# Hybrid streaming encoder on one core: post-norm scales in halves, the last tile of squares added by TensorE, the next input's first tile in halves of the tokens

## What is computed

```
def rmsnorm(x, g):
    y = xf * lax.rsqrt(jnp.mean(xf * xf, axis=-1, keepdims=True) + EPS)
    return y * g
# trunk_layer
    h = rmsnorm(x, g_norm[0])            # norm 0
    ...                                  # three mixing branches, gates
    x = x + rmsnorm(merged @ w_out, g_norm[1])   # norm 3 of the kernel
    h = rmsnorm(x, g_norm[2])                    # norm 4
    ...                                  # cross-attention into 256 memory tokens
    x = x + rmsnorm(ox @ w_xo, g_norm[3])        # norm 5
    h = rmsnorm(x, g_norm[4])                    # norm 6
    u = jnp.square(jax.nn.relu(h @ w_up)) @ w_down
    x = x + rmsnorm(u, g_norm[5])                # norm 7
```

## Time and profile before

| | |
|---|---|
| median of 3 runs | 2743.57 us (2743.19 to 2744.48) |
| profiled execution, its own time | 2743.87 us |
| its span | 2742.0 us |
| mean granted TensorE clock | 0.966 |
| PE busy | 2551.7 us (93%) |
| PEld busy | 2386.0 us (87%) |
| DVE, ACT, POOL busy | 1045.0, 707.3, 1210.9 us |

### The profile page before, as it was taken

How to read it: one execution, slowest core, us unless ns; L and a number is a source line. 1 busy time by engine, 2 the same in 40 slices (tenths; PEclk the granted TensorE clock), 3 DMA queues, 4 the chain that set the end, 5 groups by cost and what they waited for, 6 DMA issues and landing times.

```text
span 2742.0 us, 43279 instructions
## 1 busy us (share of the span) xinstructions
PE 2551.7 (93%) x18670; PEld 2386.0 (87%) x18670; DVE 1045.0 (38%) x1596; ACT 707.3 (26%) x1571; POOL 1210.9 (44%) x700
## 2 busy tenths in 40 slices
PE   8899999998988899999998999999998887999997
PEld 7878977997888789999898789689888887999997
DVE  5442222478623341221373411324786144211223
ACT  2053133135312430010121522322253134210111
POOL 3312510665465245665543034126643732565663
PEclk9999999999999999999999999999999998999998
DMA  5313410330242123323234133113202421223321
GB/s 178 111 38 102 109 41 16 85 90 24 77 125 85 39 62 88 91 85 89 81 101 120 39 89 91 42 32 85 74 24 93 130 80 32 77 85 89 90 85 56
DMA packets 354533, 214.59 MB, mean 78 GB/s; under 512 B 22316, under 2 KB 347240, under 8 KB 353704
## 3 DMA queue, kind: packets, MB, share of 16 engines
q1 hardware_dynamic: 320632, 179.86, 23.1%
q10 hardware_dynamic: 33712, 31.97, 3.7%
HBM read 196.09 MB, written 15.71 MB: 77 GB/s over the span
## 4 chain that ended last, share of the span: by engine, by line
PE 83%; DVE 8%; ACT 4%; issue 3%; POOL 2%; DMA 0%; ACTq 0%; SPq 0%; DVEq 0%; POOLq 0%
PE psum L719 20%; PE psum L717 20%; PE psum L718 20%; PE psum L788 2%; PE psum L827 2%; PE psum L729 2%; PE psum L1110 1%; PE psum L998 1%; POOL w_lo L652 1%; PE psum L921 1%; PE psum L747 1%; PE psum L749 1%; PE psum L748 1%; DVE square_sum_and_rs L2020 1%; PE psum L762 1%
## 5 line engine op out<-in xcount | busy, mean ns | idle before, releaser
L650 POOL CAST w_hi<-w_raw 128x1024 fp32r<-128x1024 f32 x318 | 337.7, 1062 | 1382.5 <-PE psum L719 1204.9
L652 POOL TENSOR_TENSOR w_lo<-w_raw,w_hi 128x1024 fp32r<-128x1024 f32 x318 | 811.6, 2552 | 25.5
L717 PE MATMUL psum<-h_hi,w_hi 128*128 128x272 f32 x2720 | 791.1, 291 | 18.9 <-POOL w_lo L652 15.1
L719 PE MATMUL psum<-h_hi,w_lo 128*128 128x272 f32 x2720 | 788.4, 290 | 0.0
L718 PE MATMUL psum<-h_lo,w_hi 128*128 128x272 f32 x2720 | 783.8, 288 | 0.0
L717 PEld LDWEIGHTS psum<-h_hi,w_hi 128*128 128x128 f32 x2720 | 513.9, 189 | 24.0 <-issue 20.9
L718 PEld LDWEIGHTS psum<-h_lo,w_hi 128*128 128x128 f32 x2720 | 514.4, 189 | 0.7 <-issue 0.5
L719 PEld LDWEIGHTS psum<-h_hi,w_lo 128*128 128x128 f32 x2720 | 512.8, 189 | 0.0
L717 PE MATMUL psum<-r_hi,w_hi 128*128 128x272 f32 x1696 | 494.2, 291 | 6.2 <-DVE hE L2114 3.3
L719 PE MATMUL psum<-r_hi,w_lo 128*128 128x272 f32 x1696 | 495.8, 292 | 0.0
L718 PE MATMUL psum<-r_lo,w_hi 128*128 128x272 f32 x1696 | 491.8, 290 | 0.0
(11 more groups left out here) (380 smaller groups left out, 3593.7 us busy)
## 6 DMA issues: line engine op xcount, KB each, us to landing
w_raw<-in_w_in SPq DMA_DIRECT2D x116, 512.0 KB, 3.8
w_raw<-in_w_up SPq DMA_DIRECT2D x64, 512.0 KB, 4.0
w_raw<-in_w_down SPq DMA_DIRECT2D x64, 512.0 KB, 3.9
w_raw<-in_w_branch SPq DMA_DIRECT2D x24, 512.0 KB, 3.4
w_raw<-in_w_out SPq DMA_DIRECT2D x16, 512.0 KB, 3.9
x_kept<-x SPq DMA_DIRECT2D x2, 2176.0 KB, 8.9
x<-x_kept SPq DMA_DIRECT2D x2, 2176.0 KB, 9.7
fKc<-in_cache_fox_k ACTq DMA_DIRECT2D x4, 1024.0 KB, 7.8
```

Source lines behind the costliest of these rows:

```text
L650: nc.gpsimd.tensor_copy(w_hi[:, at % SPLIT, :], raw[:, at % RAW, :]).then_inc(high_split, 1)
L652: nc.gpsimd.tensor_tensor(w_lo[:, at % SPLIT, :], raw[:, at % RAW, :], w_hi[:, at % SPLIT, :].bitcast(F32), ALU.subtract).then_inc(weights ...
L717: pe.matmul(dst, whi[:, k, :], hi[:, k, c0:c1], start=k == 0, stop=False)
L719: last = pe.matmul(dst, wlo[:, k, :], hi[:, k, c0:c1], start=False, stop=k == kt - 1)
```

## The change

A unit is now a tile of x, or half of tile 0: `UNITS` has 9 of them (NU), tile 0 in two halves of 272 tokens and seven whole tiles. The counts of `x_ready`, `h_hi_ready` and `h_lo_ready` and the offsets XG0 to H_PARTS follow. `POSTS` names the norms of the outputs.

1. For norms 3, 5 and 7 DVE adds the squares of tiles 0 to 6. TensorE adds tile 7 with two more products by the ones, into the same banks, after it has multiplied `acc`.
2. For the same norms ACT makes Ln and Exp of the first half of the tokens and then of the second, and `rs_ready` counts each.
3. `post`, `x_parts`, `x_low` and `norm_products` take tile 0 in halves. ACT squares tile 0 whole, after its second half. This holds for the first input of the program (norm 0 of layer 0) too.

```diff
+        UNITS = [(0, slice(0, HALF)), (0, slice(HALF, NT))] + [(t, slice(0, NT)) for t in range(1, KT)]
+        NU = len(UNITS)
+        POSTS = (3, 5, 7)
+        RS_AT = [k + 1 + sum(j <= k for j in POSTS) for k in range(len(NORMS))]
...
-        SQUARES = {0: S["sqx"], 4: sq, 6: sq}
+        SQUARES = {0: S["sqx"], 3: sq, 4: sq, 5: S["sqx"], 6: sq, 7: S["sqx"]}
...
-            for t in range(KT):
-                pe.wait_ge(h_lo_ready, since(h_lo_ready, base + t + 1))
+            for u, (t, tokens_of) in enumerate(UNITS):
+                pe.wait_ge(h_lo_ready, since(h_lo_ready, base + u + 1))
                 for name, G, (whi, wlo) in zip(names, banks, split):
                     for a in range(2):
                         c = slice(a * HALF, (a + 1) * HALF)
+                        if not tokens_of.start <= c.start < tokens_of.stop:
+                            continue
...
-                if t < KT // 2:
+                if u and t < KT // 2:
                     square_tile(pe, k, t)
...
         def stat(pe, k):
             pe.wait_ge(square_sum_ready, since(square_sum_ready, k + 1 - sum(j < k for j in PE_SUMS)))
+            whole = k not in POSTS
             for a in range(2):
                 dst = bank_free(pe, ("stat", k, a))
-                pe.matmul(dst[:, 0:HALF], ones, acc[:, a * HALF:(a + 1) * HALF], start=True, stop=True) \
-                    .then_inc(fill_sem(("stat", k, a)), 1)
+                last = pe.matmul(dst[:, 0:HALF], ones, acc[:, a * HALF:(a + 1) * HALF], start=True, stop=whole)
+                if whole:
+                    last.then_inc(fill_sem(("stat", k, a)), 1)
+            if not whole:
+                pe.wait_ge(square_ready, since(square_ready, SQ0[k] + KT))
+                for a in range(2):
+                    pe.matmul(bank_of(("stat", k, a))[:, 0:HALF], ones, SQUARES[k][:, KT - 1, a * HALF:(a + 1) * HALF],
+                              start=False, stop=True).then_inc(fill_sem(("stat", k, a)), 1)
...
-                emptied(act, ("stat", k, 1)), emptied(act, ("stat", k, 0))
-                exp(rs, acc, scale=-0.5).then_inc(rs_ready, 1)
+                    if k in POSTS:
+                        emptied(act, name)
+                        exp(rs[:, a * HALF:(a + 1) * HALF], acc[:, a * HALF:(a + 1) * HALF], scale=-0.5) \
+                            .then_inc(rs_ready, 1)
...
-                v.wait_ge(rs_ready, since(rs_ready, k + 1))
-                for t in range(KT + 2):
-                    if t < KT:
+                for i in range(NU + 2):
+                    if i < NU:
+                        t, c = UNITS[i]
+                        if i < 2:
+                            v.wait_ge(rs_ready, since(rs_ready, RS_AT[k] - 1 + i))
                         n[0] += 1
-                        V.scalar_tensor_tensor(tmp[:, t, :], U[:, t, :], gT(gcol + t, gcol + t + 1), rs,
+                        V.scalar_tensor_tensor(tmp[:, t, c], U[:, t, c], gT(gcol + t, gcol + t + 1), rs[:, c],
                                                ALU.mult, ALU.mult).then_inc(vector_chain, 1)
...
-                square_add(v, 7, S["sqx"], KT - 1)
```

More of the change, by code:

```diff
@@ L486, in hybrid_encoder @@
         PER_LAYER = [
-            (square_ready, sum(NORMS)), (square_sum_ready, len(NORMS) - len(PE_SUMS)), (rs_ready, len(NORMS)),
-            (h32_ready, KT), (h_hi_ready, H_PARTS), (h_lo_ready, H_PARTS), (x_ready, 3 * KT),
+            (square_ready, sum(NORMS)), (square_sum_ready, len(NORMS) - len(PE_SUMS)), (rs_ready, RS_AT[-1]),
+            (h32_ready, KT), (h_hi_ready, H_PARTS), (h_lo_ready, H_PARTS), (x_ready, 3 * NU),
             (cqn_ready, 1), (rope_ready, 3), (row_max, 68), (sample_probs, 4), (o_hi_ready, 19),
@@ L1259, in rs_of @@
                                          bias=eps[:, 0:1], scale=1.0 / features).then_inc(empty_sem(name), 1)
-                emptied(act, ("stat", k, 1)), emptied(act, ("stat", k, 0))
-                exp(rs, acc, scale=-0.5).then_inc(rs_ready, 1)
+                    if k in POSTS:
+                        emptied(act, name)
+                        exp(rs[:, a * HALF:(a + 1) * HALF], acc[:, a * HALF:(a + 1) * HALF], scale=-0.5) \
+                            .then_inc(rs_ready, 1)
+                if k not in POSTS:
+                    emptied(act, ("stat", k, 1)), emptied(act, ("stat", k, 0))
+                    exp(rs, acc, scale=-0.5).then_inc(rs_ready, 1)
             def h_high(act):
@@ L1269, in x_parts @@
             def x_parts(act, k, base, gcol, hi):
-                for t in range(KT):
+                for u, (t, c) in enumerate(UNITS):
                     if base is not None:
-                        act.wait_ge(x_ready, since(x_ready, base + t + 1))
-                    nc.scalar.activation(hi[:, t, :], x[:, t, :], ACT.Copy, scale=gT(gcol + t, gcol + t + 1)) \
+                        act.wait_ge(x_ready, since(x_ready, base + u + 1))
+                    nc.scalar.activation(hi[:, t, c], x[:, t, c], ACT.Copy, scale=gT(gcol + t, gcol + t + 1)) \
                         .then_inc(h_hi_ready, 1)
+                    if u == 0:
+                        continue
                     nc.scalar.activation(SQUARES[k][:, t, :], x[:, t, :], ACT.Square).then_inc(square_ready, 1)
@@ L1672, in layer @@
                 emptied(act, ("vec",), l=l - 1 if l else "in")
-                x_parts(act, 0, -KT if l else None, V_NORM, r_hi)
+                x_parts(act, 0, -NU if l else None, V_NORM, r_hi)
                 rs_of(act, 0, D_MODEL)
@@ L1706, in square_sum @@
             def square_sum(v, k, tiles):
-                for t in range(1, NORMS[k]):
+                for t in range(1, NORMS[k] - (k in POSTS)):
                     square_add(v, k, tiles, t)
@@ L1955, in dve_mla @@
                         gate(v, "kpe")
-                    v.wait_ge(rs_ready, since(rs_ready, k + 1))
+                    v.wait_ge(rs_ready, since(rs_ready, RS_AT[k]))
                     for t in range(nt):
@@ L2133, in dve_cross @@
                 post(v, 3, V_NORM + KT, sq, XG4, V_NORM + 2 * KT, h_hi, h_lo, layer_now[0])
-                v.wait_ge(rs_ready, since(rs_ready, 5))
+                v.wait_ge(rs_ready, since(rs_ready, RS_AT[4]))
                 for m in range(4):
@@ L2147, in dve_mlp @@
                 v.wait_ge(DMA["out"], since(DMA["out"], 32))
-                v.wait_ge(rs_ready, since(rs_ready, 7))
+                v.wait_ge(rs_ready, since(rs_ready, RS_AT[6]))
                 for g in range(MLP_GROUPS):
@@ L2256, in _ @@
                 layer_now[0] = DEPTH - 1
-                pe.wait_ge(x_ready, since(x_ready, 2 * KT + 4 * c + 4))
+                pe.wait_ge(x_ready, since(x_ready, 2 * NU + 4 * c + 5))
                 layer_now[0] = "out"
@@ L2301, in _ @@
             layer_now[0] = 0
-            for t in range(KT):
+            for t in range(NU):
                 x_low(v, t, XG0, V_NORM, r_hi, r_lo, 0)
```

25 lines of the change are left out of this document (14 added, 11 removed).

## The result

| | before | changed |
|---|---|---|
| median, 16 runs each | 2744.35 us (2742.53 to 2745.64) | 2740.04 us (2737.41 to 2743.44) |
| profiled execution, its span | 2743.87, 2742.0 us | 2739.10, 2737.2 us |
| mean granted clock | 0.966 | 0.970 |

The ratio is 0.9985 with a 95% interval of 0.9978 to 0.9992. The change is worth 4.3 us, where I forecast 10.4; the time lies above my range.

What follows compares the result with a forecast made beforehand. TensorE, busy 93% of the span, was taken as the bound, so only its idle time and slow stretches could be won: 5.3 + 1.6 + 3.9 + 0.1 + 0.2 - 0.7 = 10.4 us, giving 2733.2 us, range 2729.5 to 2738.5.

Steps and rivals of the forecast that it cites:

- norm 5, each: Norm 5, twice: tile 0's products end 2.65 us earlier, with DVE held by POOL's subtraction; 3.35 without the hold.
- norm 3, each: Norm 3, twice: the halves end tile 0 about 0.8 us earlier, though memory copies and `post` start 0.92 later.
- norm 7, layer 0: Norm 7 of layer 0: the held 2.75 us addition goes and halves shorten the restart; gain 3.9 us, between 3.2 and 4.7.
- norm 7, layer 1: Norm 7 of layer 1: two more products and the halves' cost about offset the earlier scale; +0.1 us, between -1.0 and +0.3.
- start: The program's first input: half of the held first low part ends sooner; +0.2 us, between 0 and 0.5.
- held multiplication: DVE multiplication beside POOL's subtraction, taken to last until POOL ends; in norm 5 the first half multiplication ends at 961.9.
- rival (b): DVE not held in norm 5 (0.7 us more per layer), norm 7's sums at full clock (0.8): 2731 us; chance 0.14.
- rival (c): Half tiles cost almost as much as wholes (0.70 and 0.64 us), gain 4.4 us: 2739 us; chance 0.05.
- The slow stretch: TensorE at 1.2 GHz after five restarts, the clock rising 3.5 to 4.9 us behind each; -0.7 us, 2 each way.
- Rival (d): Piecewise starts delay the clock's rise at all five restarts and eat the gain: 2738 to 2743 us; chance 0.09.

Runs made afterwards that it cites:

- e10: The changed kernel, but in norm 3 DVE adds the last tile of squares again, scale and tile 0 staying in halves: 2734.16 us, ratio 0.9963.
- e15: The kernel of e10, unaltered, profiled in a second execution: 2734.77 us, span 2733.0.
- e5: The kernel before, with TensorE multiplying constants (40 products, results overwritten) in its waits ahead of the six inputs' products: 2735.44 us, ratio 0.9972.
- e6: The changed kernel with TensorE multiplying constants in its waits (43 products, results overwritten): 2730.36 us, ratio 0.9957.
- e14: The kernel before, unaltered, profiled in a second execution: 2745.72 us, span 2743.9.
- e1: The kernel before, with five extra whole-tile additions on DVE ahead of its first low part: 2747.36 us, ratio 1.0010.
- e2: The kernel before, with three extra whole-tile additions on DVE ahead of its first low part: 2745.77 us, ratio 1.0005.
- e7: The changed kernel with three extra whole-tile additions on DVE at the start: 2742.97 us, ratio 0.9998 against the kernel before.

## Why the prediction was wrong

Tile 0's end counted from the last product, by the terms of the prediction:

| term | forecast | at tile 0's end | left behind the stage |
|---|---|---|---|
| norm 5, each | 2.65 | 2.49 | 1.3, 1.2 |
| norm 3, each | 0.8 | 0.46 | 0.4, 0.2 |
| norm 7, layer 0 | 3.9 | 4.2 | 4.9 |
| norm 7, layer 1 | +0.1 | 0 | 0 |
| start | +0.2 | 0.5 | 0.5 |
| sum without the clock | 11.1 | 10.6 | 8.6 |
| clock | -0.7 | | -2.0 of it above, -3.8 elsewhere |

**Right.** Norm 5 ran by the chain that I wrote down: scale at 960.35 (forecast 960.3), the two held multiplications to 962.22 (962.3), TensorE at 964.18 (964.25). The held multiplication, which I had inferred from one sum and one low part, is shown: 1.84 us for two halves, until 0.71 us behind POOL's end, and rival (b) with its 0.7 is out for norm 5. The Trainium skill states the ground in "GPSIMD Engine Reference", section "1. Specifications": GpSimd's SBUF interfaces are shared with VectorE, which contends for them when an instruction has two SBUF inputs. The rows agree. The half widths were right too, 0.42 and 0.35 in the chains, so rival (c) is out. The copies in norm 3 came 0.92 later.

**Sizes.** Making tile 0 in two pieces cost TensorE 0.3 us. The second low part came in time (TensorE went on at 965.83, forecast 966.0), but the first product behind a break takes 0.55 in the chain, and I had taken 0.227; that is what norm 5 and norm 3 lack. Only in norm 7 of layer 0 did TensorE stand idle between the halves, 0.33 us. There the sums ran at full clock (the 0.8 us of rival (b)), and the clock rose again 3.9 us after the restart (1369.3 to 1373.2) instead of 4.9, which is why the stage kept more than tile 0 gained. That was luck: in e10, with the same code there, it rose 5.8 us after the restart, and the stage kept 0.9 less. Of the 0.5 at the start none can be told from the 0.8 by which two executions of one kernel differ there.

**The step that failed** is "The slow stretch", the term of -0.7. It was -5.8. Two us went at the restarts, in the way that the term describes: at norm 5 the earlier restart did not bring an earlier rise, which came 6.2 and 6.4 us behind it and not 3.5 to 4.9. The loss was what I had for every rise at 4.9. It isn't owed to the halves: in e10 and e15, with the same code at norm 5, the rise came 3.2 to 3.5 us behind the restart. The 3.8 I had no term for. I priced the clock at five restarts, as if only idle time brought it down and only those restarts could change. But it fell at 25 to 28 places in each execution without filling, in the changed kernel at three of them with TensorE busy all the time, and at which of the weak places it falls differed between kernels, and between two executions of one. Rival (d) named the right thief, and its 4 to 10 us the right amount, by the wrong mechanism and at 0.09.

**What is shown and what not.** That slow stretches and not a wait took the 5.8 us is shown for the profiled executions, by the windows and the table. TensorE's time over the whole span says the same: idle time fell by 14.0 us, of which 5.5 are the new products' own time, and 7.1 us more of busy time fell into slow stretches (127.2 to 134.3), 3.6 us lost: 14.0 - 5.5 - 3.6 = 4.9, against 4.8 measured. This loss is below 5.8 since it is net: 4.7 us of the kernel before's sums behind norms 5 and 7 of layer 0 and norm 5 of layer 1 ran slow, and now run at full clock, which the table counts as a gain of the norms. e5 and e6 show that the clock is worth twice the change, but not that the change would give its 11 us without it (5.1). That the parts don't add (4.7, 5.0, together 4.3) has two causes: 2.2 us of it are in the waits, at norm 5 by POOL's hold, and the rest in these stretches. How large the loss is in the mean over executions isn't: against e14's trace the changed kernel gains 6.7 us of span, against the first 4.8, while the medians of 16 runs differ by 4.3. Nor did the runs give a rule for where the clock falls; a bare delay left the falls of the kernel before where they were in the program (e1, e2) and moved those of the changed kernel (e7). The Trainium skill, "TensorE: Matmul & The Clock Gate", section "What's actually happening", ties the clock to how busy TensorE has lately been and says, of the rise at a kernel's start, that its point varies from run to run. The falls vary too: the first of the same kernel came at 18.1 and at 20.0 us. The first half does not cover 236.6 us, where TensorE was busy 2.00 of 2.00 us.

## What to carry to other kernels

When TensorE sets the time and its granted clock falls and rises along the run, sum up a change at the waits it shortens, and then put a term with its own wide range on the clock over the whole program: here it was more than half of the gain. Count stretches where TensorE is busy with narrow products among its risks, not the waits alone. Before naming a cause from two profiles, profile each kernel once more. A new instruction on TensorE ahead of something another engine waits for (the transposes in norm 3) is paid in every layer even where its sum is free: giving that one part back made the best kernel without filling, 2734.2 us, though the waits explain only 1.3 of its 5.9 us. Under a hold, an engine that is ready earlier gains nothing until the other engine is through. Where waits for a norm are left, products of constants in them can be worth more (here 8.6 us on the kernel before) than shortening them.

## What the hardware did that I had not expected

- The granted clock fell to 0.50 with TensorE busy all the time, behind products with 8 rows or 64 columns, 3.0 us lost each time; and behind the same products it stayed at 1.00 in the first profile of the kernel before.
- The same kernel has such a stretch in one execution and not in another (2742.0 against 2743.9 us of span), and from norm 3 of layer 0 on its clock falls at the same places of the program in both.
- Two held multiplications ended 0.71 us behind POOL's subtraction as halves and 1.28 as wholes.
- A restart 2.76 us earlier did not bring the clock's rise forward (970.42 us, before 970.40), though in e10 it rose 3.5 us behind the same restart.
